# Pooling means on GpSimd during attention, merge gates on GpSimd's queue, and two merge tiles in alternation

## The reference

```python
u_pool, q, kv, nsa_g, merge_g = split(rms_norm(x) @ w_in)
# pool mixer: 4 groups of 128 channels, windows 2, 4, 8, 16
pooled[g][t] = mean(u_pool[g][max(0, t+1-w) : t+1]) - u_pool[g][t]
y_pool = ((pooled @ pool_w) * pool_scale) @ w_pool_br
y_attn = nsa_attention(q, k, v, nsa_g, ...) @ w_attn_br
merged = sigmoid(merge_g)[0] * y_pool + sigmoid(merge_g)[1] * y_attn
x = x + merged @ w_o
```

## Time and profile before

| | us |
|---|---|
| runs, median (lowest to highest) | 2092.08 (2075.64 to 2093.07) |
| span of the profiled execution | 2089.5 |
| TensorE busy | 1837.3 (88%) |
| VectorE busy | 1019.7 (49%) |
| ScalarE busy | 775.2 (37%) |
| GpSimd busy | 41.2 (2%) |

### The profile page before, as it was taken

How to read it: one execution, slowest core, us unless ns; L and a number is a source line. 1 busy time by engine, 2 the same in 40 slices (tenths; PEclk the granted TensorE clock), 3 DMA queues, 4 the chain that set the end, 5 groups by cost and what they waited for, 6 DMA issues and landing times.

```text
span 2089.5 us, 23598 instructions
## 1 busy us (share of the span) xinstructions
PE 1837.3 (88%) x8490; PEld 1468.4 (70%) x8490; DVE 1019.7 (49%) x1657; ACT 775.2 (37%) x1358; POOL 41.2 (2%) x57
## 2 busy tenths in 40 slices
PE   5897599999888799998989978888997997798987
PEld 4777577777667688886767775557874666577966
DVE  5234466566545565663234335664363234534654
ACT  3122144443322455552132125554253442315651
POOL 0001000000000000000000000000000000000001
PEclk8898599999989899999999998898997778898998
DMA  7320001111233233332322230010321011211111
GB/s 181 90 74 27 0 29 43 60 60 48 91 101 121 60 100 100 83 89 81 101 75 81 85 102 1 21 41 21 116 82 40 21 41 37 70 61 41 41 41 40
DMA packets 157156, 135.74 MB, mean 65 GB/s; under 512 B 9744, under 2 KB 151440, under 8 KB 156944
## 3 DMA queue, kind: packets, MB, share of 16 engines
q1 hardware_dynamic: 154032, 126.89, 20.4%
q0 software_dynamic: 1600, 5.24, 0.7%
q10 hardware_dynamic: 1440, 2.50, 0.4%
HBM read 127.28 MB, written 7.34 MB: 64 GB/s over the span
## 4 chain that ended last, share of the span: by engine, by line
PE 77%; DVE 12%; issue 4%; ACT 3%; DMA 2%; SPq 2%; DVEq 0%; ACTq 0%
PE bank L294 18%; PE bank L295 17%; PE bank L296 17%; PE bank L992 3%; PE bank L963 2%; PE bank L976 2%; DVE wlo L287 2%; PE bank L2108 1%; PE bank L476 1%; PE bank L883 1%; PE bank L2472 1%; ACT whi L280 1%; DVE ssn L443 1%; PE bank L1674 1%; PE bank L2094 1%
## 5 line engine op out<-in xcount | busy, mean ns | idle before, releaser
L294 PE MATMUL bank<-hh,whi 128*128 128x512 f32 (+2 forms) x1104 | 450.1, 408 | 37.2 <-DVE hl L415 20.3
L295 PE MATMUL bank<-hl,whi 128*128 128x512 f32 (+2 forms) x1104 | 439.7, 398 | 0.0
L296 PE MATMUL bank<-hh,wlo 128*128 128x512 f32 (+2 forms) x1104 | 439.1, 398 | 0.0
L280 ACT ACTIVATE whi<-wraw 128x2048 fp32r<-128x2048 f32 x112 | 213.9, 1911 | 398.1 <-PE bank L296 388.2
L287 DVE TENSOR_TENSOR wlo<-wraw,whi 128x2048 fp32r<-128x2048 f32 x112 | 256.2, 2288 | 199.3 <-ACT whi L280 197.9
L294 PEld LDWEIGHTS bank<-hh,whi 128*128 128x128 f32 (+2 forms) x1104 | 211.2, 191 | 98.9 <-issue 25.6
L296 PEld LDWEIGHTS bank<-hh,wlo 128*128 128x128 f32 (+2 forms) x1104 | 211.3, 191 | 48.0
L295 PEld LDWEIGHTS bank<-hl,whi 128*128 128x128 f32 (+2 forms) x1104 | 212.0, 192 | 43.3 <-issue 1.7
L1016 DVE COPY pt<-bank 128x128 f32<-128x128 f32 (+2 forms) x96 | 42.6, 469 | 105.6 <-PE bank L976 105.5
L294 PE MATMUL bank<-ah,whi 128*128 128x512 f32 x192 | 77.1, 402 | 12.3 <-DVE al L2607 8.5
L1026 ACT ACTIVATE pr<-bank,nm 128x128 f32<-128x128 f32 (+3 forms) x128 | 66.2, 529 | 45.8 <-DVE nm L1082 45.7
(11 more groups left out here) (354 smaller groups left out, 3106.1 us busy)
## 6 DMA issues: line engine op xcount, KB each, us to landing
wraw<-in_w_in_a_dram SPq DMA_DIRECT2D x52, 512.0 KB, 4.5
wraw<-in_w_up_dram SPq DMA_DIRECT2D x42, 512.0 KB, 4.7
wraw<-in_w_in_dram SPq DMA_DIRECT2D x34, 512.0 KB, 4.7
wraw<-in_w_in_c_dram SPq DMA_DIRECT2D x18, 512.0 KB, 4.4
wraw<-in_w_down_dram SPq DMA_DIRECT2D x16, 512.0 KB, 4.3
wraw<-in_w_out_a_dram SPq DMA_DIRECT2D x16, 512.0 KB, 4.3
aside<-stage POOLq DMA_DIRECT2D x20, 256.0 KB, 2.3
w<-in_cmp_w_dram SPq DMA_DIRECT2D x4, 1024.0 KB, 12.6
```

The costliest lines, as they stand in the source:

```text
L280: act.activation(whi[:, p], wraw[:, p], ACT.Copy).then_inc(w_hi_done, 1)
L294: pe.matmul(out, ws[0], hs[0], start=first, stop=False)
L295: pe.matmul(out, ws[0], hs[1], start=False, stop=False)
L296: return pe.matmul(out, ws[1], hs[0], start=False, stop=last)
```

## The change

GpSimd computes the pooling means in the attention stage, one group for each u_pool tile that ScalarE drains. ScalarE now drains these four tiles into pu (after the mean before is done), and the mean goes through `stage` to `aside`. pu, pa and rc have new places, over which ol is written later, so VectorE waits for the means before its fourth ol. In the merge GpSimd's queue loads pm, pool_w and all gates; SP's queue holds only items. TensorE accumulates the first two tiles of the attention branch in alternation, k by k. Some pairs of semaphores become one that counts on (n_root and n_rec become n_inv, and the like at four other places), with the same producers and readers.

```diff
@@ block1_attention @@
         @block.gpsimd
         def _(pool):
-            for t in range(PV_T + GATE_T):
+            pool.wait_ge(c_mm1, 2)
+            pool.dma_start(rc[:, :, :], con[:, CCOL["rcnt"]:CCOL["rcnt"] + 64].rearrange(
+                "p (g n) -> p g n", g=4)).then_inc(p_landed, 16)
+            pool.memset(pa[:, :, 0:16], 0.0)
+            pool.memset(pu[:, 0:16], 0.0).then_inc(p_pad, 1)
+            pool.wait_ge(p_landed, 16)
+            for g, wd in enumerate(POOL_WINDOWS):
+                pool.wait_ge(drained, m0 + g + 1)
+                if g:
+                    pool.wait_ge(spilled, 16 * g)
+                src, step, flip = pu, 1, 0
+                while step < wd:
+                    to = pa[:, flip, :]
+                    gch(pool, pool.tensor_tensor(to[:, 16:16 + S], src[:, 16:16 + S], src[:, 16 - step:16 + S - step],
+                                                 ALU.add))
+                    src, step, flip = to, 2 * step, 1 - flip
+                pool.tensor_tensor(stage[:, 0:16], src[:, 16:32], rc[:, g, :], ALU.mult)
+                gch(pool, pool.tensor_scalar(stage[:, 16:S], src[:, 32:16 + S], 1.0 / wd, 1.0, ALU.mult, ALU.mult))
+                gch(pool, pool.tensor_tensor(stage[:, :], stage[:, :], pu[:, 16:16 + S], ALU.subtract))
+                pool.sem_inc(p_mean, 1)
+                pool.dma_start(aside[g], stage[:, :]).then_inc(spilled, 16)
+            for t in range(PV_T, PV_T + GATE_T):
                 pool.wait_ge(drained, m0 + t + 1)
                 pool.dma_start(aside[t], stage[:, :]).then_inc(spilled, 16)
...
                     act.wait_ge(tiles, 2 * n0 + t + 1)
-                    if t:
+                    if t < PV_T:
+                        act.wait_ge(p_pad, 1)
+                        if t:
+                            act.wait_ge(p_mean, t)
+                        act.activation(pu[:, 16:16 + S], bank[7][:, :], ACT.Copy).then_inc(drained, 1)
+                    else:
                         act.wait_ge(spilled, 16 * t)
-                    act.activation(stage[:, :], bank[7][:, :], ACT.Copy).then_inc(drained, 1)
+                        act.activation(stage[:, :], bank[7][:, :], ACT.Copy).then_inc(drained, 1)
...
                     p = u // 4 - 1
+                    if p == 3:
+                        dve.wait_ge(p_mean, PV_T)
@@ block1_merge @@
+            for i in range(MI):
+                items(i)
+
+        @block.gpsimd
+        def _(pool):
             def gates(i):
-                if i:
-                    sp.wait_ge(g_full, AHEAD + 4 * i)
                 for part in range(2):
                     t0 = PV_T + KT * part + 2 * i
-                    sp.dma_start(gs[:, 2 * part:2 * part + 2, :], aside[t0:t0 + 2].rearrange("t p n -> p t n")) \
-                        .then_inc(got_x, 16)
+                    pool.dma_start(gs[:, 2 * part:2 * part + 2, :], aside[t0:t0 + 2].rearrange("t p n -> p t n")) \
+                        .then_inc(g_landed, 16)
-            items(0)
-            sp.wait_ge(spilled, 16 * (PV_T + GATE_T))
-            sp.wait_ge(pv_done, UNITS)
-            sp.dma_start(pu[:, :, 16:16 + S], aside[0:PV_T].rearrange("t p n -> p t n")).then_inc(got_con, 16)
-            sp.dma_start(pw[:, :, :], w["pool_w"].rearrange("g c d -> c g d")).then_inc(got_con, 16)
-            sp.dma_start(rc[:, :, :], con[:, CCOL["rcnt"]:CCOL["rcnt"] + 64].rearrange(
-                "p (g n) -> p g n", g=4)).then_inc(got_con, 16)
+            pool.wait_ge(spilled, 16 * (PV_T + GATE_T))
+            pool.wait_ge(s_done, 4 * UNITS)
+            pool.dma_start(pm[:, :, :], aside[0:PV_T].rearrange("t p n -> p t n")).then_inc(p_landed, 16)
+            pool.dma_start(pw[:, :, :], w["pool_w"].rearrange("g c d -> c g d")).then_inc(p_landed, 16)
+            pool.wait_ge(pv_done, UNITS)
             gates(0)
             for i in range(1, MI):
-                items(i)
+                pool.wait_ge(g_full, AHEAD + 4 * i)
                 gates(i)
...
-                for t in range(2):
+                if i == 0:
                     for k in range(KT):
-                        if i == 0 and t == 0:
-                            pe.wait_ge(o_out, k + 1)
-                        mm = passes(...)
-                    mm.then_inc(tiles, 1)
+                        pe.wait_ge(o_out, k + 1)
+                        for t in range(2):
+                            mm = passes(...)
+                            if k == KT - 1:
+                                mm.then_inc(tiles, 1)
+                else:
+                    for t in range(2):
+                        tile_of(pe, a, t, bank[c + t][:, :], (oh, ol)).then_inc(tiles, 1)
                 if i == 0:
-                    pe.wait_ge(got_con, CON_P)
+                    pe.wait_ge(p_landed, 48)
...
-                act.wait_ge(got_x, 16 * TT + 32 * (i + 1))
+                act.wait_ge(g_landed, 32 * (i + 1))
```

More of the change, by code:

```diff
@@ L911, in two_blocks @@
     spilled = sem("spilled")
+    pu = at("pu", Y + 6 * K, [16 + S])
+    pa = at("pa", Y + 8 * K + 512, [2, 16 + S])
+    rc = at("rc", Y + 13 * K, [4, 16])
+    p_pad, p_mean, p_landed, g_landed = sem("p_pad"), sem("p_mean"), sem("p_landed"), sem("g_landed")
+    gch = Chain("pool_own")
     PIECES = 4 * (PV_T + GATE_T)
@@ L1181, in _ @@
                 item_ready(pe, a)
[L1182 removed]
+                if i == 0:
                     for k in range(KT):
[L1184 to L1189 removed]
+                        pe.wait_ge(o_out, k + 1)
+                        for t in range(2):
+                            mm = passes(pe, bank[c + t][:, :], (whi[:, a % 2, k, P * t:P * t + P],
+                                                                wlo[:, a % 2, k, P * t:P * t + P]),
+                                        (oh[:, k, :], ol[:, k, :]), k == 0, k == KT - 1)
+                            if k == KT - 1:
[3 more added lines that the diff above has]
+                        tile_of(pe, a, t, bank[c + t][:, :], (oh, ol)).then_inc(tiles, 1)
                 if i == 0:
[L1191 removed]
+                    pe.wait_ge(p_landed, 48)
                     pe.wait_ge(t_act, UNITS)
@@ L1224, in _ @@
         def _(dve):
-            dve.wait_ge(p_pad, 1)
-            dve.wait_ge(got_con, CON_P)
-            for g, wd in enumerate(POOL_WINDOWS):
-                src, step, flip = pu[:, g, :], 1, 0
-                while step < wd:
-                    dst = pa[:, flip, :]
-                    dch(dve, dve.tensor_tensor(dst[:, 16:16 + S], src[:, 16:16 + S], src[:, 16 - step:16 + S - step],
-                                               ALU.add))
-                    src, step, flip = dst, 2 * step, 1 - flip
-                dch(dve, dve.tensor_tensor(pm[:, g, 0:16], src[:, 16:32], rc[:, g, :], ALU.mult))
-                dch(dve, dve.tensor_tensor(pm[:, g, 0:16], pm[:, g, 0:16], pu[:, g, 16:32], ALU.subtract))
-                dch(dve, dve.scalar_tensor_tensor(out=pm[:, g, 16:S], in0=src[:, 32:16 + S], scalar=1.0 / wd,
-                                                  in1=pu[:, g, 32:16 + S], op0=ALU.mult, op1=ALU.subtract))
-                dve.sem_inc(p_mean, 1)
             for i in range(MI):
@@ L1635, in _ @@
         def _(pe):
-            pe.wait_ge(l_prod, 1)
-            pe.matmul(bank[4][:, 0:2], ones[:, :], lprod[:, :], start=True, stop=True).then_inc(l_sum, 1)
-            pe.wait_ge(l_lam, 1)
+            pe.wait_ge(l_step, 1)
+            pe.matmul(bank[4][:, 0:2], ones[:, :], lprod[:, :], start=True, stop=True).then_inc(l_step, 1)
+            pe.wait_ge(l_step, 4)
             pe.wait_ge(drained, m1)
@@ L2035, in two_blocks @@
     hfb = at("hfb", SC_AT + 14 * K, [2, S])
[L2036 to L2037 removed]
+    z_silu, z_prod, z_sq, z_add, z_sum, z_inv, z_spread, z_full, z_high, z_low = (
+        sem(n_) for n_ in ("z_silu", "z_prod", "z_sq", "z_add", "z_sum", "z_inv", "z_spread", "z_full",
                            "z_high", "z_low"))
```

90 lines of the change are left out of this document (37 added, 53 removed).

## The result

The changed kernel took 2065.67 us in the median of 12 runs (2055.53 to 2083.68), the kernel before, run side by side with it, 2076.54 us (12 runs, 2070.37 to 2093.46; the three listed at the start are among them). The ratio is 0.9916, with an interval of 0.9888 to 0.9944: faster by 0.6 to 1.1%. The medians are 11 us apart and the means 15 (2066.7 and 2082.1). Only part of that is work saved, as the experiments show.

The account below looks back on a forecast made before the run. TensorE, 77% of the span, was taken as the bound, idle while waiting for operands in the merge. 14 us gained there less 3 lost in the attention takes 11 off 2092.08: 2081 us, forecast 2075 to 2087, wider range 2064 to 2093.

Parts of the forecast that it names:

- Pooling out of the merge: Merge's pool stage: pm loaded ready-made, pool-branch tiles start 7.5 us earlier; 9.4 us in all with the clock staying high.
- Gates on GpSimd's queue: Merge rounds: weight loads no longer stand behind gates, so ScalarE's waits of 4.5 us go.
- X: Merge, each round: time from the gates' issue at the sums to the sigmoid's start; taken as 5.4 us, range 3.8 to 9.2.
- Alternation and semaphores: First two merge tiles accumulated in alternation, and merged semaphores: claimed to gain nothing.
- Means in the attention: Attention stage: GpSimd's operations slow VectorE; 3 us lost in the third mean, 0 to 8 for all.
- The sum: Whole kernel: 14 us gained in the merge less 3 lost in the attention, 11 us off, giving 2081.
- Rival A: Attention: every GpSimd operation holds up VectorE and TensorE in all four means, 26 us less the 14: 2104; chance 0.06.
- rival B: Merge: gates' loads slow on GpSimd's queue, 9.2 us each round; 2.7 gained, 3 lost: 2092, no change; chance 0.11.
- C: Rival: gates land early in the merge and the attention loses nothing; 19 us gained, 2073; chance 0.18.
- D: Rival: merge's pool stage is gone but another wait is as long; 2089; chance 0.10.
- The stages behind shift as a whole.: Stages after the merge: claimed to move earlier together, with no gain or loss of their own.
- a stage behind 700 that changes its own length: Listed sign of being wrong: a stage later than 700 us in the profile changing its duration; no size given.

Follow-up runs that it names:

- the second trace: The changed kernel run once more, unchanged, beside the kernel before; median 2066.6 us over 10 runs, ratio 0.9916.

## Why the prediction was partly right

**Pooling out of the merge: right.** Forecast 7.5 us, measured 7.6 (25.8 to 18.2), with each step in its place and the clock at its upper level. The experiment without means shows what the prediction did not separate: half of it is that u_pool, pool_w and the constants no longer stand ahead of the first gates and weights on SP's queue.

**Gates on GpSimd's queue: right in mechanism, mis-sized.** ScalarE's waits for weight loads vanished. X was 5.85, 6.8 and 5.9 us instead of 5.4, which takes 2.3 us over three rounds (1.2 in the second trace), and by undoing it the part is worth 3.2 us in M instead of 4.5. Together with the pool stage M fell by 12.3 us (11.3 in the second trace) against 14 forecast.

**Behind the merge: a term that was missing.** TensorE's first wait for ml grew from 2.1 to 3.3 us in the w_o projection, and in the profiled execution the clock fell there, so W was 2.8 us longer; in the second trace both were as before (2.1 and 53.0). The prediction took this stage as unchanged.

**Alternation and semaphores: right**, nothing each.

**Means in the attention: right in mechanism, mis-sized.** Forecast 3 us in the third mean, measured 1.3 at TensorE there and 1.6 to 1.8 in all. The query halves and the scalings, 0.9 us each, are where the prediction put them, but it is one instruction of each that waits, and the product in between lost nothing (0.17 us in both kernels). The prediction spread 0.39 us over seven instructions; what the rows show are two meetings there, and one in the fourth mean that costs nothing. The Trainium skill ("SBUF — State Buffer", section "Who interferes with whom") says that whoever issues first keeps the shared pair of ports for the whole instruction and the other is blocked. The trace agrees: one of two query halves took 1435 ns against 811, and GpSimd's add beside wlo 2142 against 1.03 us for the same add in the fourth mean. The 8 us that I had worked out from that rule were wrong by the number of meetings, not by the rule.

**The sum:** 14 - 3 = 11 forecast to the next norm, 7.8 and 9.5 measured (447.2 to 439.4, 446.5 to 437.0). That the medians are 11 us apart as well is luck: 1.4 to 3.1 of those 11 come from elsewhere, and the means are 15 apart. The 15 us between the predicted 2081 and the measured 2066 come from the starting point: the forecast took 2092.08, the median of three runs, and the median of twelve is 2076.54. Rival A is refuted by A at 303.7; rival B by the loads of 5.9 to 6.8 us; C asked for M 19 us shorter; D asked for a wait about as long as the old one, and the two that came are 1.7 us each.

**The step that failed:** "The stages behind shift as a whole." They don't. The state-space stage took a different rhythm more often. Side by side the means are 15.4 and 16.4 us apart (2082.1 to 2066.7, 2082.6 to 2066.3), and some 6 to 9 of them are left when the 7.8 to 9.5 up to the next norm are taken off. The runs show that adding 1.3 us to the kernel before moves its mean by 9.6 us down, so a gain of that size can be had there without pooling or queues. That this is also how the changed kernel got its gain is the likeliest reading and not shown: adding to it or taking from it went with 9 and 8 us more, but not side by side. The prediction did name "a stage behind 700 that changes its own length" as a sign of being wrong, and gave it no chance and no price. The three runs of before (2092, 2093, 2076) lay at two levels 17 us apart, which was the hint: the prediction took it as noise of the measurement, and started from the upper level.

**A second step, the bar:** that 1% is what a measurement of this kernel can tell was too coarse. Twelve runs of each gave an interval of 0.3% to either side, so even the forecast 11 us (0.5%) would have stood out as faster. The weight on "no change" followed from that bar and not from the sum.

**Left open:** which moments of entry give the quick rhythm, and whether it is the moment at all or the place of the instructions in the program. One, two and three added instructions gave means 5.8, 9.6 and 2.1 us below the kernel before beside them, with errors of 3.8, 1.9 and 2.2, which is no simple rule. It was not tried to give the stage itself work in its idle stretches, which might make the quick rhythm certain.

## What to carry to other kernels

Work moved to an idle engine can pay twice, once for the work and once for the loads that no longer stand ahead of others on a queue; tell the two apart by leaving the work out and keeping the loads where they are. A change of queue is worth what the next thing on that chain lets it be: here 3 us alone with the pooling gone, nothing without it, and 7 us more only once the gates had a second buffer. When a kernel's runs fall into two groups, find the stage whose length differs and compare stage by stage, and run both kernels side by side, since such a stage can be worth as much as the change under study.

## What the runs showed of the hardware

The same eight rounds, with the same instructions, took 97 to 117 us, at a granted clock of 0.96 or 0.79 with the other engines' busy time unchanged. One unchanged program showed both 104 and 117, and with two useless instructions of 0.66 us ahead of the stage the mean time fell by 9.6 us, with one or three by no amount clear of the noise. GpSimd's two-input add on 128x512 took 1.03 us alone and 2.14 when it began beside VectorE's wlo, whose own 2.28 did not change, while VectorE's first scaling waited for GpSimd's subtraction: who pays depends on who was first, and it waits for the other's end. A pair of 512 KB loads on GpSimd's queue took 1.42 us to issue and 5.6 to 6.8 us from the release to the first use (two traces), against 5.1 to 5.6 on SP's (kernel before and gates on SP's queue).
